# Residual additions of ten K tiles as accumulating transfers in a streaming-encoder block on one core

## The reference

```python
h = rmsnorm(x, norm_mix_pre)
y = hybrid_mixer(h, ...)                 # ends with @ w_out
x = x + rmsnorm(y, norm_mix_post)        # the residual addition
h = rmsnorm(x, norm_ffn_pre)
y = conv_gated_mlp(h, ...)               # h @ w_gate, h @ w_up, convolution, gelu, product, @ w_down
x = x + rmsnorm(y, norm_ffn_post)
```

## Time and profile before

| | |
|---|---|
| median of three runs | 2129.07 us |
| profiled execution | 2130.63 us |
| its span, first to last instruction | 2128.8 us |
| PE, weight loads | 2118.0 us (99%), 2088.7 us (98%) |
| VectorE | 1691.6 us (79%) |
| ACT | 1027.6 us (48%) |
| GpSimd | 353.6 us (17%) |
| granted TensorE clock, mean | 0.999 |
| chain that ended last | PE 97%, VectorE 2% |

### The profile page before, as it was taken

How to read it: one execution, slowest core, us unless ns; L and a number is a source line. 1 busy time by engine, 2 the same in 40 slices (tenths; PEclk the granted TensorE clock), 3 DMA queues, 4 the chain that set the end, 5 groups by cost and what they waited for, 6 DMA issues and landing times.

```text
span 2128.8 us, 44315 instructions
## 1 busy us (share of the span) xinstructions
PE 2118.0 (99%) x18226; PEld 2088.7 (98%) x18226; DVE 1691.6 (79%) x2316; ACT 1027.6 (48%) x1305; POOL 353.6 (17%) x448
## 2 busy tenths in 40 slices
PE   9999999999999999999999999999999999999999
PEld 8999999999999999999999999999999999999998
DVE  7777767777855889888888888888887867767887
ACT  5665554456422455444444444444454545445443
POOL 1222322222100001212112121121211001011102
PEclk9999999999999999999999999999999999999999
DMA  5689997989543437887878878778888658679645
GB/s 178 153 200 207 201 203 190 199 194 200 151 129 99 146 124 220 224 225 206 224 214 224 225 205 225 215 223 221 227 223 273 197 162 282 186 190 273 219 139 189
DMA packets 239571, 424.90 MB, mean 200 GB/s; under 512 B 17312, under 2 KB 152352, under 8 KB 238128
## 3 DMA queue, kind: packets, MB, share of 16 engines
q0 software_dynamic: 88896, 160.49, 36.5%
q1 hardware_dynamic: 147920, 257.37, 36.2%
q10 hardware_dynamic: 2592, 4.72, 0.6%
HBM read 383.69 MB, written 89.16 MB: 222 GB/s over the span
## 4 chain that ended last, share of the span: by engine, by line
PE 97%; DVE 2%; issue 1%; ACT 1%; POOL 0%; DVEq 0%; ACTq 0%; POOLq 0%
PE bank L2173 30%; PE bank L2175 30%; PE bank L2174 30%; PE bank L2571 2%; PE bank L2265 1%; PE bank L2252 1%; PE bank L2277 0%; PE bank L2276 0%; PE bank L2340 0%; PE bank L2292 0%; ACT w_all L823 0%; DVE tsum_f L2148 0%; PE bank L2229 0%; PE bank L2358 0%; PE bank L2357 0%
## 5 line engine op out<-in xcount | busy, mean ns | idle before, releaser
L2173 PE MATMUL bank<-act_hi,w_all 128*128 128x256 f32 x3216 | 894.2, 278 | 0.9 <-DVE act_lo L1298 0.6
L2175 PE MATMUL bank<-act_hi,w_all 128*128 128x256 f32 x3216 | 888.3, 276 | 0.0
L2174 PE MATMUL bank<-act_lo,w_all 128*128 128x256 f32 x3216 | 888.2, 276 | 0.0
L2173 PEld LDWEIGHTS bank<-act_hi,w_all 128*128 128x128 f32 x3216 | 603.7, 188 | 8.2 <-issue 5.1
L2174 PEld LDWEIGHTS bank<-act_lo,w_all 128*128 128x128 f32 x3216 | 603.8, 188 | 0.3 <-issue 0.2
L2175 PEld LDWEIGHTS bank<-act_hi,w_all 128*128 128x128 f32 x3216 | 603.7, 188 | 0.0
L2173 PE MATMUL bank<-tsum,w_all 128*128 128x256 f32 x1312 | 362.8, 277 | 0.7 <-issue 0.7
L2175 PE MATMUL bank<-tsum,w_all 128*128 128x256 f32 x1312 | 362.1, 276 | 0.0
L2174 PE MATMUL bank<-tsum,w_all 128*128 128x256 f32 x1312 | 362.1, 276 | 0.0
L1150 ACT ACTIVATE w_all<-raw_s 128x1024 fp32r<-128x1024 f32 x176 | 186.8, 1061 | 239.6 <-PE bank L2175 230.0
L1886 DVE TENSOR_TENSOR w_all<-raw_s,w_all 128x1024 fp32r<-128x1024 f32 x176 | 215.4, 1224 | 69.6 <-ACT w_all L1150 68.3
(11 more groups left out here) (412 smaller groups left out, 3560.5 us busy)
## 6 DMA issues: line engine op xcount, KB each, us to landing
raw<-weights SPq DMA_DIRECT2D x260, 512.0 KB, 4.4
w_sums<-weights POOLq DMA_DIRECT2D x96, 512.0 KB, 6.9
raw_s<-weights SPq DMA_DIRECT2D x86, 512.0 KB, 5.5
raw_s<-weights POOLq DMA_DIRECT2D x86, 512.0 KB, 5.8
raw_a<-weights SPq DMA_DIRECT2D x67, 512.0 KB, 5.6
raw_s<-w_sums SPq DMA_DIRECT2D x48, 512.0 KB, 5.1
t_spill<-h_out POOLq DMA_DIRECT2D x48, 256.0 KB, 3.5
act_lo_f<-t_spill POOLq DMA_DIRECT2D x11, 1024.0 KB, 9.3
```

The lines of the kernel that those rows point to most:

```text
L2173: pe.matmul(dst, ah, bh, start=start, stop=False, skip_group_check=goes_on)
L2174: pe.matmul(dst, ah, bl, start=False, stop=False, skip_group_check=goes_on)
L2175: return pe.matmul(dst, al, bh, start=False, stop=stop, skip_group_check=goes_on)
```

## The change

For the K tiles 6 to 15 the addition is no longer an instruction of VectorE. GpSimd issues a transfer from og[k] to x1[k] with `accum_op=ALU.add` instead, in a new loop ahead of its stores, each after the scaling of its tile, and ACT's high part waits for the landing. The scaling is moved two tiles ahead of the low part. The semaphores `t_landed` get another name, `tile_landed`, and four of them serve the new landings too, so the counts that later stages wait for rise by the number of tiles that each has seen.

```diff
+DMA_X1 = 6
+X1_TILES_LANDED = (2, 2, 3, 3, 0, 0, 0)
...
@@ gpsimd
+            for k in range(DMA_X1, KT):
+                pool.wait_ge(og_scaled, k + (1 if k == DMA_X1 else 2))
+                pool.dma_start(x1[:, k], og[:, k], accum_op=ALU.add).then_inc(tile_landed[k % 4], 16)
             for j in range(PLAIN - 1):
                 store_after(j)
...
@@ scalar, x1_tile
-                    act.wait_ge(x1_done, k + 2)
+                    if k < DMA_X1:
+                        act.wait_ge(x1_done, k + 2)
+                    else:
+                        act.wait_ge(tile_landed[k % 4], 16 + (k - DMA_X1) // 4 * 16)
...
@@ scalar, t_n_hi
-                act.wait_ge(t_landed[n], 16 * c + 16)
+                act.wait_ge(tile_landed[n], 16 * (c + X1_TILES_LANDED[n]) + 16)
...
@@ vector
             def x1_tile(k):
-                dve.wait_ge(og_scaled, k + 2)
+                dve.wait_ge(og_scaled, k + (3 if k == DMA_X1 - 1 else 2))
                 dve.tensor_tensor(x1[:, k], x1[:, k], og[:, k], ALU.add).then_inc(x1_done, 1)
...
             def x1_lo(k):
-                dve.wait_ge(x1_done, k + 2)
+                if k < DMA_X1:
+                    dve.wait_ge(x1_done, k + 2)
                 lo_of_scaled(k, x1, "g_ffn", 2 * KT + k)
...
-            for k in range(4, KT):
-                if k == KT - 2:
+            scale_og(4)
+            x1_tile(4)
+            x1_lo(3)
+            scale_og(6)
+            split(N_FF + 2, 0)
+            x1_lo(4)
+            scale_og(5)
+            x1_tile(5)
+            scale_og(7)
+            x1_lo(5)
+            split(N_FF + 3, 1)
+            for k in range(DMA_X1, KT):
+                if k + 2 == KT - 2:
                     dve.wait_ge(o_done, KT + 1)
                     chain(dve.tensor_scalar(og[:, KT - 1, HS:S], o1[:, HS:S], col("g_post", KT - 1), None, ALU.mult))
-                scale_og(k)
-                x1_tile(k)
-                x1_lo(k - 1)
-                if k >= 4 and k % 2 == 0:
-                    split(N_FF + k // 2, k // 2 % 2)
-            x1_lo(KT - 1)
+                if k + 2 < KT:
+                    scale_og(k + 2)
+                x1_lo(k)
+                if k % 2 and k < KT - 1:
+                    split(N_FF + (k + 1) // 2, (k + 1) // 2 % 2)
```

More of the change, by code:

```diff
@@ L357, in block_kernel @@
         s1_landed = [sem(f"s1_landed{s}") for s in range(2)]
-        t_landed = [sem(f"t_landed{n}") for n in range(7)]
+        tile_landed = [sem(f"tile_landed{n}") for n in range(7)]
         y_stored = [sem(f"y_stored{n}") for n in range(2)]
@@ L732, in load_t @@
                     pool.wait_ge(stored_t, each * m)
-                pool.dma_start(operand(NS + PAIRS_OUT * c, n)[3], t_d[c, T_PLACE[n]].rearrange("p (k n) -> p k n", n=HS)).then_inc(t_landed[n], 16)
+                pool.dma_start(operand(NS + PAIRS_OUT * c, n)[3], t_d[c, T_PLACE[n]].rearrange("p (k n) -> p k n", n=HS)).then_inc(tile_landed[n], 16)
             def store_y(i):
@@ L2568, in unsplit_product @@
                     pe.wait_ge(landed, each * (i + 1))
-                pe.wait_ge(t_landed[n], 16 * ((i - NS) // PAIRS_OUT) + 16)
+                pe.wait_ge(tile_landed[n], 16 * ((i - NS) // PAIRS_OUT + X1_TILES_LANDED[n]) + 16)
                 for k in range(UK):
```

## The result

The changed kernel takes **2133.17 us** (median of 13 runs, 2130.43 to 2135.67) against 2129.17 us before (13 runs, 2128.6 to 2130.68): a ratio of 1.0015, 95% interval 1.0008 to 1.0022. The medians differ by 4.0 us; the ratio comes to 3.2 us, 1.7 to 4.7 by its interval. That lies within the 0.2% that was called no change, and the median lies 0.2 us above the upper end of the range. The profiled execution took 2130.43 us, the fastest of the 13 and 0.2 us less than the profiled one before. Over all traces of this document that start lies between 710.0 and 712.4 us, so I compare stages and not the totals of profiled executions.

A forecast was written before the change was run, and what follows sets the result against it. PE was taken to bound the stretch. From 2130.63 us, -0.18 + 0.1 + 0 gave 2130.55 for the profiled execution; the median, 1.56 lower, was forecast at 2129.0 us, range 2128.2 to 2133.0, chance 0.58.

The forecast's parts named there:

- What bounds the kernel: Stretch of the change: PE bounds it; VectorE, busy 9.58 of 10 us, is never late; 0.18 us to gain.
- the rival of 2122.2 us: VectorE was the bound after all, so the whole 6.9 us come off; chance 0.02.
- Term 1: Before tile 4 on PE: its low part is ready earlier, so the lost time goes; -0.18 us.
- Term 2: At tile 6: VectorE's new order brings its low part level with PE's need; 0 to +0.2, taken as +0.1 us.
- Term 3: ACT's new wait at tiles 6 to 15: landings of 4.4 us stay below 4.8, costing 0.
- L: Landing time of an accumulating transfer, counted from the end of its tile's scaling; taken as 4.4 us.
- the surplus: DMA engines, ten tiles: 2.9 us asked in 2.72, 0.2 us a tile or 2 us, falling on weight loads.
- The loop and its price: Scaling, landing, ACT, VectorE over six tiles: landings may average 4.8 us; each us above costs 3.3 in ten tiles.
- landings a little late: Neighbours stretch landings to 4.8 to 6.0 us; PE waits at tiles 8, 10, 14; +2.0 us, 2131.0; chance 0.25.
- Issues held up by VectorE: VectorE delays GpSimd's accumulating issues by 1.22 us at most; landings 5.6 us, +2.6 us, 2131.6; chance 0.08.
- the rule of the Trainium skill: VectorE locks GpSimd out fully during a 2-port instruction; one tensor_scalar here could delay one issue, leaving the sum unchanged.
- DMA engines full: Stretch's transfers exceed the engines, deciding from 1.2 us an accumulation; at 1.9, +6 us, 2135 us; chance 0.07.

The follow-up runs named there:

- the covered stage: Changed kernel with x1's stores issued after the stage and scalings from tile 9 on three tiles ahead instead of two; 2128.90 us, ratio 0.9999.
- three ahead: Changed kernel with scalings from tile 9 on three tiles ahead of the low part instead of two; 2130.99 us, ratio 1.0007.
- load only: Kernel before, plus ten accumulations of 256 KB in the same stage that nobody waits for until the next stage; 2129.26 us, ratio 1.0001.

## Why the prediction was wrong

- **What bounds the kernel: right.** VectorE at 9.58 of 10 was no bound. Its 6.9 us came off it and not off the time, and the rival of 2122.2 us fell.
- **Term 1, -0.18: right.** The hole ahead of tile 4 is gone in the changed kernel, and the stage without other holes is 44.43 us.
- **Term 2, +0.1: at its lower end.** No hole ahead of tile 6 in either profile of the changed kernel.
- **Term 3 failed, at one number: "I take 3.9 + 0.5 = 4.4 us".** The base came out right, by two differences that cancel: an accumulation alone takes 3.6 and not 3.9 us, but from its issue, and 0.3 lie between the end of the scaling and the issue. The half us for the neighbours was too little. They add 1.5 to 1.7 us (medians), so L is 5.4 to 5.6, over the 4.8 that the loop bears. I had the share of the engines beside it and used it for the wrong transfers: the surplus, I wrote, "falls on the weight loads", which had 4.1 us to spare. Here everyone's landing grew: the loads lost 0.6 us of their spare time, while the accumulations, which had 4.8 - 3.9 = 0.9, lost 1.5 and more.
- **The loop and its price: right, to 0.4 us.** It asked for the average. The ten landings of the table average 5.3 and 5.55 us, so L is 5.6 and 5.85, and the loop gives 0.8 x 3.3 = 2.6 and 1.05 x 3.3 = 3.5 us; against the 44.43 us of the covered stage the two profiles lost 2.6 and 3.9.
- **The rival "landings a little late" came**, at the upper end of its 0 to +4.0, and its holes stood where it put them, ahead of tiles 8, 10 and 14. It had 0.25 of the chance; it should have been the forecast, and with a landing of 6.5 us, within the 3.7 to 9.3 of the earlier trace rows, the range would have gone past 2133.
- **Issues held up by VectorE: did not come.** 859, 862 and 897 ns, as in the earlier trace rows. In the changed kernel the one tensor_scalar of the stretch met no issue; with three ahead it ran inside one:

```profile
739.14 0.86 POOL L782 DMA_DIRECT2D x<-og  x1 [2.48 <-DVE og L1753]
739.43 0.39 DVE L1805 TENSOR_SCALAR og<-o,par 128x256 f32<-128x256 f32 x1
```

The issue took the usual 0.86 us, the tensor_scalar 0.39 instead of 0.35. No such hold-up as the rule of the Trainium skill that was quoted there speaks of shows in these rows; whether this tensor_scalar is a 2-port instruction no row tells.

- **DMA engines full: the state came, its price didn't.** 1.6 us an accumulation lies over the 1.2 us at which it was to decide, and the share is 1; but weight loads never made PE wait, not even in load only, where the same share cost nothing and they landed after 6.4 us in the middle. The price of 1.9 us at its high end was itself misread: 3.8 x 0.97 / 2 is 1.84.

That the queue of an issue gives no bandwidth of its own is what the Trainium skill says on its page "DMA: Bandwidth & Descriptors", section "Issuing engines are not separate DMA queues": transfers of ScalarE, SyncE and GpSimd run on the same 16 engines and interleave. The trace agrees: thinning ACT's stores or SP's loads shortened GpSimd's landings from 5.1 to 4.3 and 4.4 us. The same page (section "Anatomy of one DMA — SWDGE (gpsimd) path") gives 2.0 us plus the bytes at 436 GB/s, an estimate of 2.6 us for 256 KB; the accumulation alone took 3.6, so by that figure L would have been too small still.

## What to carry to other kernels

When an operation is handed to a transfer, add up first what the DMA engines are asked for in that stretch, in us a tile against the tile's time, look which of them are in flight beside the new one, and price the landing under that load, not from a quiet stretch. Then find the loop that the landing stands in: here every us above a known limit costs, and below it nothing does. And relieve an engine only where somebody waits for it: a share of 96% busy was not a wait.

## What the runs showed that was not expected

A longer lead lengthened the landing itself (5.1 to 6.5 and 6.6 us) probably because more of them are then in flight at once; more lead alone did not cover it, less traffic and more lead together did. An accumulating issue keeps GpSimd 0.86 us, a plain one of the same shape 0.54 (all ten at 536 to 538 ns). The DMA share of a window can read above 1 (1.09 from 730 to 740 us with three ahead), so near 1 it does not tell what is left.
